# Three more places in the ring of gathered rows, paid for by a smaller descriptor scratch

## The reference

```python
eidx = i1 * PEER_N_KEYS + i2            # (64 tokens, 8 heads, 16 of 16384 experts)
g = jax.nn.softmax(cs, axis=-1)
u = expert_u[eidx]                      # 128 rows of 1024 floats for each token
v = expert_v[eidx]
act = gelu(einsum('td,thkd->thk', xb, u))
out = einsum('thk,thkd->td', (g * act), v)
```

## Time and profile before

| | before |
|---|---|
| time of three runs, median (lowest to highest) | 2529.69 us (2524.82 to 2530.29) |
| span of the profiled execution, first to last instruction | 2410.2 us |
| TensorE matmul busy | 2170.0 us (90%) |
| VectorE busy | 1511.6 us (63%) |
| GpSimd busy | 1015.5 us (42%), 1024 gathers |
| moved by DMA | 831.37 MB, of which 536.94 MB by the gathers |

### The profile page before, as it was taken

The page is one execution under the profiler, slowest core; times in us unless marked ns, Lnnn a source line. Parts: engine busy times, 40 slices in busy tenths (PEclk is TensorE's granted clock), DMA queues, the critical chain, the costliest instruction groups (busy, mean ns, idle before and its releaser), DMA issues.

```text
span 2410.2 us, 29349 instructions
## 1 busy us (share of the span) xinstructions
PE 2170.0 (90%) x10850; PEld 1522.1 (63%) x10850; DVE 1511.6 (63%) x3509; ACT 638.7 (26%) x1797; POOL 1015.5 (42%) x1028
## 2 busy tenths in 40 slices
PE   8999999999999999889697784389889999999998
PEld 7999886666666798777552273133366655446695
DVE  3442159999999737986828398920077768876321
ACT  6673235555555413000200010010122000001310
POOL 0000003555566411464557765757644647661000
PEclk9999999999999999999899977689998999999999
DMA  6666746999999896999999999999999999998484
GB/s 239 216 220 234 269 185 232 377 386 378 364 377 351 310 380 252 402 408 413 411 408 408 409 370 411 410 354 410 411 381 357 412 412 412 412 412 361 143 336 162
DMA packets 191983, 831.37 MB, mean 345 GB/s; under 512 B 21456, under 2 KB 21712, under 8 KB 160096
## 3 DMA queue, kind: packets, MB, share of 16 engines
q0 software_dynamic: 147456, 536.94, 57.0%
q1 hardware_dynamic: 43808, 290.72, 31.7%
q10 hardware_dynamic: 576, 1.84, 0.2%
HBM read 827.31 MB, written 2.10 MB: 344 GB/s over the span
## 4 chain that ended last, share of the span: by engine, by line
PE 60%; DVE 17%; DMA 12%; POOL 4%; issue 4%; ACT 3%; DVEq 0%; ACTq 0%
PE ps L1169 59%; DVE rows L2692 9%; DMA rows<-in_pu,eidx 5%; DMA rows<-in_pv,eidxT 5%; POOL rows L1141 4%; DMA wr<-in_wgate 1%; DVE arena L2245 1%; ACT arena L1696 0%; DVE rows L2159 0%; DVE h L2716 0%; PE ps L1554 0%; PE ps L1306 0%; DMA wr<-in_wso 0%; DVE rows L2157 0%; DVE ps L2716 0%
## 5 line engine op out<-in xcount | busy, mean ns | idle before, releaser
L1141 POOL DMA_INDIRECT rows<-in_pu,eidx x512 | 484.8, 947 | 840.6 <-DVE arena L2245 362.5
L1169 PE MATMUL ps<-arena,wr 128*128 128x128 f32 (+4 forms) x3968 | 762.4, 351 | 19.6 <-DVE arena L2348 9.4
L1169 PEld LDWEIGHTS ps<-arena,wr 128*128 128x128 f32 x3968 | 600.8, 193 | 161.8 <-issue 21.2
L2692 DVE CUSTOM_DVE_ANT_0 rows<-rows,ps 128x1024 f32<-128x1024 f32 x512 | 603.0, 1217 | 51.8 <-DMA rows<-in_pu,eidx 46.6
L1141 POOL DMA_INDIRECT rows<-in_pv,eidx x256 | 285.8, 1117 | 195.1 <-DVE h L2716 117.2
L1169 PE MATMUL ps<-hT,wr 128*128 128x128 f32 (+2 forms) x1600 | 353.1, 382 | 5.0 <-DVE xx L2542 2.9
L1169 PEld LDWEIGHTS ps<-hT,wr 128*128 128x128 f32 x1600 | 255.2, 194 | 99.5 <-issue 3.8
L1141 POOL DMA_INDIRECT rows<-in_pv,eidxT x256 | 244.7, 956 | 131.9 <-issue 64.1
L1169 PE MATMUL ps<-rows,wz 128*32 128x512 f32 x1024 | 212.6, 616 | 50.0 <-DMA rows<-in_pv,eidxT 48.5
L2716 DVE SCALAR_TENSOR_TENSOR h<-rows,wgt,h 128x1024 f32<-128x1024 f32 x132 | 169.1, 1281 | 26.3 <-DMA rows<-in_pv,eidx 25.3
L1169 PE MATMUL ps<-wr,arena 128*128 128x256 f32 (+2 forms) x704 | 181.7, 414 | 0.0
(11 more groups left out here) (398 smaller groups left out, 2277.6 us busy)
## 6 DMA issues: line engine op xcount, KB each, us to landing
wr<-in_wg SPq DMA_DIRECT2D x48, 1024.0 KB, 6.4
wr<-in_wgu SPq DMA_DIRECT2D x33, 1024.0 KB, 8.1
wr<-in_wgate SPq DMA_DIRECT2D x24, 1024.0 KB, 7.5
wr<-in_wso SPq DMA_DIRECT2D x24, 1024.0 KB, 8.1
wr<-in_wq SPq DMA_DIRECT2D x16, 1152.0 KB, 8.1
wr<-in_wsc SPq DMA_DIRECT2D x16, 1024.0 KB, 6.1
wr<-in_wqku SPq DMA_DIRECT2D x15, 1024.0 KB, 8.1
wr<-in_wdn SPq DMA_DIRECT2D x14, 1024.0 KB, 8.0
```

What stands on the lines that cost most here:

```text
L1141: e.indirect_dma_start(ring[slot_of[i]], None, A[table], bass.IndirectOffsetOnAxis(ap=index[:, t, k:k + 1], axis=0)).then_inc(gathered[slo ...
L1169: return e.matmul(o, l, r, start=start, stop=stop, skip_group_check=True)
L2692: e.tensor_tensor_reduce(row, row, wide[:], 1.0, 0.0, MUL, ADD, dots[:, k:k + 1]).then_inc(*dve.up(*u))
```

## The change

Three things are edited. The descriptor scratch gets 4096 bytes per partition in place of 16384. The 12288 bytes that come free are three places of 4096 bytes: `NR` goes from 13 to 16 and `NR0` from 8 to 11. The new places are 8, 9 and 10; `side` moves up from places 8 to 12 to places 11 to 15, with the same size. And the order in which the early places are first used starts with the four that hold no weights.

```diff
-NR = 13
+NR = 16
@@
-NR0 = 8
+NR0 = 11
@@ in build()
-        slots, user, slot_of, before_of, value_of = [7, 5, 6, 0, 1, 2, 3, 4], {}, [], [], []
+        slots, user, slot_of, before_of, value_of = [7, 8, 9, 10, 5, 6, 0, 1, 2, 3, 4], {}, [], [], []
@@ in kernel()
-    nc = bacc.Bacc("TRN2", target_bir_lowering=False, num_devices=1)
+    nc = bacc.Bacc("TRN2", target_bir_lowering=False, num_devices=1, dynamic_dma_scratch_size=4096)
```

## The result

| chip | kernel before, us | changed kernel, us | ratio, 95% interval |
|---|---|---|---|
| that of the timed runs | 2527.34 (2519.82 to 2530.29) | 2538.51 (2531.64 to 2544.29) | 1.0046, 1.0026 to 1.0067 |
| chip 9 | 2514.76 (2506.66 to 2526.66) | 2524.74 (2516.72 to 2527.86) | 1.0030, 1.0017 to 1.0043 |
| chip 14 | 2409.55 (2405.22 to 2414.70) | 2396.82 (2391.86 to 2397.68) | 0.9938, 0.9924 to 0.9952 |

The forecast was 12.1 us less. The measured answer is 11 us more. The third row is the key: there are chips on which the same unchanged kernel takes about 2410 us and chips on which it takes 2515 to 2530. I call them quick and slow chips. On a quick chip a gain of the forecast size is there, 12.7 us. The ratios are not quotients of the medians beside them: by its ratio the gain on chip 14 is 14.9 us, and the loss on chip 9 is 7.5 us where the medians give 10.0.

The account below looks back on a forecast made before the run. No single engine bounds it: DMA is full at about 411 GB/s in stretches, with gaps where no ring place was free. Terms 0.7 + 3.8 + 3.8 + 3.8 = 12.1 us off 2529.7 gave 2517.6 us, range 2512 to 2530.

Parts of the forecast that it names:

- The sum: Whole kernel: 0.7 + 3.8 + 3.8 + 3.8 = 12.1 us off the profiled span and equally off the median.
- the gaps: Idle DMA time near 951, 1385, 1600 and 1825 us: 1.4, 4.4, 6.8 and 5.4 us, partly closed by three more places.
- The last gap counted: At 1825 us, 5.4 us idle: rows three places earlier bring 3.8 us, bounds 0 and 3.83.
- 3.8 us a gap: At 1385, 1600 and 1825 us: three more gathers of 1.276 us each gain at most 3.83 us per gap.
- The close of the tiles: VectorE's normalization ending each tile: tile 1 closes 0.7 us earlier, tile 2 8.3, the last gather comes 12 earlier.
- TensorE's stall before the down products: Before 2085.55 us: rows three places earlier shorten this stall from 5.43 us to about 1.6.
- GpSimd's stops: Idle 7.60 us after 1386.01 and 12.18 us after 1593.39 for a free place; three more gathers go out first.
- The range: Whole kernel: from 2512 us (17 us of gain, all bounds plus tile 0) to 2530 us, no gain.
- the 2 us of tile 0: From 362 us: three more early places may bring 0 to 2 us; taken as 0.
- GpSimd's price for a gather: At each gather: still 0.94 us with 0.30 us behind it, so the smaller scratch costs nothing.
- rival 1: Rows come early but another engine takes the gain; all is lost, 2529.7 us; chance 0.13.
- The rival on the slower side: GpSimd pays for the small scratch at each gather, 0.1 us more over 455 gathers: 2547.6 us; chance 0.11.

Follow-up runs that it names:

- after_again: The changed kernel once more, unedited, against the kernel before on chip 14 (quick): 2396.82 against 2409.55 us, ratio 0.9938.
- scratch_1024: The kernel before with its 13 places and a descriptor scratch of 1024 bytes, on chip 14 (quick): 2409.99 us, ratio 1.0001.
- late_16_d: The changed kernel with eight early places and 16 afterwards, scratch 4096, against the kernel before on chip 11 (quick): 2400.92 against 2409.58 us, 0.9966.
- before_again: The kernel before, no edit, against itself on chip 7 (slow): 2533.18 against 2527.37 us, ratio 1.0025.
- late_16_c: The changed kernel with eight early places and 16 afterwards, scratch 4096, against the kernel before on chip 9 (slow): 2520.96 us, 1.0019.

## Why the prediction was wrong

**The step that failed** is "The sum": "The median of the runs lies 119.5 us above the profiled span, and nothing of the change touches what lies around it". The difference was an unexplained 5%, and I took it as a constant outside the program. It is inside: the span is 2525.1 us for 2410.2, with about 100 us of halts, more TensorE busy time (2206.9 for 2170.0 us) and a lower clock (0.933 for 0.952). All rows were from an execution without halts, and every term of the sum assumes that TensorE, once its rows are there, runs. On the chip of the timed runs that is where it fails: the changed kernel waits only 17.2 us for rows there, and has 126.4 us of halts, and it takes 11 us more, not 12.1 less.

**Point by point**, on quick chips:
- DMA time idle in the gaps, by length x (1 - share/1.02) from the fences above, before to after_again: 945 to 975 us, 3.8 to 2.6; 1370 to 1410, 4.3 to 0.8; 1575 to 1615, 6.7 to 1.2; 1730 to 1780, 2.9 to 0.5; 1810 to 1850, 5.5 to 5.5. The first two answer to 0.7 and 3.8 of the forecast. The third gave 5.5 for 3.8. The last gap counted gave nothing; one that I had not counted, round 1765 us, gave 2.4. The five add up to 12.6 us, beside 12.7 measured, but not by the terms that I had written, and that the sums agree is luck. scratch_1024, a ring of 13, has 4.1, 1.2, 5.9, 3.4 and 2.0 in the same windows, 16.6 us in all; from it to after_again (10.6) only 6.0 us close. late_16_d, 16 late places, has 4.1, 0.4, 7.1, none and 7.1 us: its gaps at 1600 and 1825 did not close at all, and it still gained 8.7 us. So the terms of the sum can't be read from one trace of each, and 3.8 us a gap is not confirmed gap by gap.
- The close of the tiles (VectorE's normalization, L2734), before to after_again: tile 0 925.95 to 923.12, tile 1 1384.40 to 1380.35, tile 2 1755.07 to 1740.89, tile 3 2202.22 to 2184.70. That is 2.8, 4.1, 14.2 and 17.5 us, for 0, 0.7, 8.3 and 12. scratch_1024 closes them at 928.11, 1388.77, 1757.47 and 2201.05, so executions with the same ring differ by 1 to 4 us. late_16_d has 923.68, 1382.71, 1747.69 and 2192.85: with eight places its tile 0 closes as early as with eleven, which leaves nothing in these traces that is the early places' for certain. By medians the whole gain is 12.7.
- TensorE's stall before the down products: 5.43 to 0.76 us, forecast 1.6. This sign holds in more traces: 4.17 us in scratch_1024, 0.76 us in late_16_d. GpSimd's stops: 7.60 to 6.26 and 12.18 to 8.06; the second is 12.38 in late_16_d, so it is no sign of the ring.
- The range: the bounds of the sum and the 2 us of tile 0 give 1.4 + 3 x 3.83 + 2 = 14.9 us of gain, 2514.8 us, and not the 17 us and 2512 that I wrote.
- GpSimd's price for a gather: 938 ns in the median, 0.30 us behind it, as forecast. Scratch: no time, down to 1024 bytes (1.0001), though with 1024 only some 7 gathers are in flight (scratch_1024 above). How many 4096 bytes hold no run shows. In after_again, which has them and 16 places, GpSimd's issue waits are 181.9 us in 594, the longest 0.6 us as in before, so there is no sign that they limit anything.

**On slow chips** rival 1, "another engine takes the gain", comes nearest: it named VectorE and TensorE by their place in the plan's order and gave 2529.7 us, no change. It was TensorE, but by halts, which no rival had, and the kernel takes up to 11 us more instead of less. The rival on the slower side had the wrong mechanism. "A time above 2535 us would refute the sum and point to the scratch": it refuted the sum for this chip, and the scratch had no part in it.

How sure is the sign on slow chips? Over the three groups that ran there the 16-place kernels came out at 1.0046, 1.0030, 1.0036 and 1.0019; the others (the kernel before itself, small scratch, ring of 8 at the end, early places alone) at 1.0025, 1.0018, 1.0002, 1.0021 and 0.9981. All runs of a chip taken together, without the timed group, say it closer: on chip 7 the mean of the 12 runs with 16 late places lies 6.8 us (3.3 to 10.3) above that of the 69 others, on chip 9 the mean of 24 lies 7.6 us (4.9 to 10.4) above that of 57. So a loss of some 7 us goes with the rings of 16; the kernel before differs from itself by nearly as much on chip 7 (5.8 us by medians). Why it comes out as a loss and not as no change isn't shown.

No version was seen to beat the kernel before on both kinds. On quick chips the changed kernel is the best of all that ran with the whole computation; on slow chips none was faster than the kernel before by more than a kernel differs from itself there.

## What to carry to other kernels

If the timed median and the profiled span lie percents apart, find out where before adding up anything: the trace may be of an execution that behaves otherwise than the timed ones. Here a deeper ring turned waits into bursts (VectorE's dots in 15.00 of 15 us with 16 places, in 10.04 with 8). On the quick chips that paid (79 us from 8 places to 13, 12.7 from 13 to 16), on chips 7 and 9 TensorE was held back in turn (40.6 us of halts with 8 places, 105.4 with 13, 116.2 with 16). And the value of a place fell steeply with depth (81, 16, 3 to 4 us a place here), so a change of the last few places is worth no more than what two chips of one kind differ by (2527 and 2515 us), and a ninth of what the two kinds differ by.

## What the runs showed of the hardware

- The same program takes 2410 us on chips 14 and 11 and 2515 to 2527 on 9 and 7. The DMA peak is the same (413 and 412 GB/s in the earlier trace rows and the page after), and so is GpSimd's gather to 4 ns (937 and 941 ns). The traces of before and before_again differ in TensorE's issue waits (5.9 and 103.1 us) and its granted clock (0.952 and 0.933).
- Halts come in the midst of a row of like products (`ps<-hT,wr` and `ps<-lf,con` from 1500 to 1537 us in before_again). There are 91 in that trace, 70 of them with 0.6 to 2.6 us each. In the long series the matmuls between them start on multiples of 0.70 us from each other (1514.53, 1517.34, 1520.13: 2.81 and 2.79 us, four times 0.70). They are told as "issue", of which the chain that ended last has 6% in before_again and in the changed kernel's trace, 4% in before. In the stretches of the long series the granted clock is 0.57 (before_again, 1500 to 1522 us), 0.63 and 0.70 (late_16_c, 1060 to 1073 and 2007 to 2020 us); before each of them it was 1.00.
- Descriptor scratch: against 16384 bytes, 4096 give 1.0018 (0.9997 to 1.0039, chip 7) and 1024 give 1.0001 (0.9988 to 1.0014, chip 14), with a ring of 13 places and gathers of 128 rows of 4 KB. With 1024 bytes a gather lands 12.6 us after its issue in the median (27 of them, 1044 to 1090 us), with 16384 20.3 us (32 of them), and GpSimd's longest issue wait is 2.8 us for 0.6.
